# Un-normed inputs for the first projections and the query projection, and split passes for the retention products, in a two-block fp32 kernel

## The chip, the cores and the metric

One core of a Trainium2 chip. The metric is the time of one launch in device microseconds (us), the median of three runs. Engines are called by the profile's names: PE (TensorE), ACT (ScalarE), DVE (VectorE), POOL (GpSimd), SP (SyncE, which here only issues transfers).

## The reference

256 tokens of width 1024 go through two blocks. Cut to what the change touches:

```python
# first block
n1 = rmsnorm(h, norm1_g)                 # h / sqrt(mean(h*h) + eps) * gain
q, k, v, r, a_lr, su, sv, ga, gb = split(n1 @ w_in)
...                                      # gated linear attention, spatial gating, merge
h = h + merged @ w_out
n2 = rmsnorm(h, norm2_g)
q = (n2 @ w_q)                           # 8 heads x 2 halves x 128
s1, s2 = q[:, :, 0] @ sub_k1.T, q[:, :, 1] @ sub_k2.T
...                                      # top 16 of each, top 16 of the sums, experts, h = h + peer(n2)
# second block: two feed-forward layers around a retention layer with 4 heads
sc = einsum('id,jd->ij', q, k) * decay   # 256 queries, 512 keys (context and own), d = 256
o  = einsum('ij,jv->iv', sc, v)          # v is 512 wide
```

## The kernel before, in words

All weights are one stream of chunks of 128 x 1024 fp32 (512 KB), in the order of the table `ORDER`. SP loads chunk c into one of four slots of RAW (`load`, L372). A product with fp32 operands is computed in three passes: each operand is the sum of a part rounded to `float32r` (names with H) and the rest (names with L), and PE adds H*H, H*L and L*H (`product`, L1555 to L1557). So each chunk is split before use: ACT rounds it (`split_hi`, WH, L479) and DVE subtracts (`split_lo`, WL, L944; from the query projection to the experts POOL does it instead, `pool_lo`, L427). `split_hi(c)` waits for chunk c-4 on PE, `split_lo(c)` for `split_hi(c)`, SP's next load of the slot for `split_lo`. Every engine runs its own list in order and waits on semaphores; there is no planner.

A `feature_chunk` (24 matmuls with 256 columns) has the weights stationary and gives 128 features of 256 tokens, accumulated in one PSUM bank over the eight 128-row blocks k. A `token_chunk` (12 matmuls with 512 columns, L1586 to L1588) has the tokens stationary; four of them fill K, V or the gating input SV in token direction. A third form, in the experts, doubles the columns.

**Norm.** ACT squares the eight blocks (L482), PE sums them with a matrix of ones in eight plain fp32 matmuls (`norm_sum`, L1595), ACT takes the root (L486), DVE the reciprocal (L949), and then block by block DVE scales (L952), ACT rounds (L493, XH) and DVE subtracts (L959, XL). The PE's first product needs block 0 of this.

**Start.** After the norm: chunk "alr" (features), twelve token chunks "tok" (K, V, SV), then 28 feature chunks "feat" with pieces of the attention between them (`glu`). **Query projection.** "wout" (8 feature chunks, in a loop, each added to H by DVE), norm, "wq" (16 feature chunks in four loop rounds, each evicted to QT, then two small fp32 matmuls, `scores`, L1696), then "pre" (32 expert rows) beside a long top-k chain on DVE, whose result is turned by PE before the 29th of these chunks (L1743). **Retention heads.** Per head 14 chunks; between them eight plain fp32 matmuls with 256 columns for the scores (L1925), the decay on DVE (PT), and eight plain fp32 matmuls with 512 columns for the values (L1936).

## Time and profile before

| | us |
|---|---|
| median of 3 runs (lowest, highest) | 2168.5 (2166.01, 2171.08) |
| profiled execution, its own time | 2167.95 |
| its span, first to last instruction | 2166.1 |
| PE busy | 2101.8 (97%) |
| DVE, ACT, POOL busy | 1198.6, 1019.0, 132.2 |
| mean granted clock of PE | 0.99 |

The span is what the rows below are measured in; 1.85 us lie around it. PE's matmuls are pipelined: a row's duration reaches beyond the start of the next, so the step from start to start is what one costs. An idle time in brackets is that of the engine just before the row, with what ended it.

### The profile page before, as it was taken

To read this page: it belongs to the slowest core of one execution; us is meant where nothing else is said; L and a number is where in the kernel's file an instruction comes from. 1 tells how busy PE (TensorE), PEld (TensorE's weight loads), DVE (VectorE), ACT (ScalarE), POOL (GpSimd) and SP (SyncE) were. 2 spreads that over 40 slices of the span, in tenths; PEclk is the share of its full clock that TensorE was granted. 3 is DMA by queue.
4 is the path that set the end of the run, shared out by engine and by line. 5 is a ranking of instruction groups with operands and counts; after the bars stand their busy time and mean duration, and the time that the engine had idled before them with its cause. 6 is when DMAs were issued, how large, how long until landed. Compare 5 with 4: busy or idle time off the path is not lost.

```text
span 2166.1 us, 35548 instructions
## 1 busy us (share of the span) xinstructions
PE 2101.8 (97%) x12650; PEld 1825.6 (84%) x12650; DVE 1198.6 (55%) x2044; ACT 1019.0 (47%) x1538; POOL 132.2 (6%) x72
## 2 busy tenths in 40 slices
PE   8999998899999999999999999999999999999997
PEld 6899898778888888888888888887888888899996
DVE  4456794796666666666665333224544534355554
ACT  4644444675555555555554222213433434336753
POOL 0000567100000000000000000000000000000001
PEclk9999999999999999999999999999999999999999
DMA  6435356696555555565552233322323335254563
GB/s 214 138 127 175 117 204 207 237 324 222 191 191 187 189 186 189 189 204 191 187 167 102 96 95 96 115 95 75 107 88 116 97 137 184 88 190 140 182 195 117
DMA packets 95232, 343.91 MB, mean 159 GB/s; under 512 B 10962, under 2 KB 11474, under 8 KB 94772
## 3 DMA queue, kind: packets, MB, share of 16 engines
q1 hardware_dynamic: 93908, 337.28, 46.9%
q0 software_dynamic: 1248, 5.57, 0.7%
q8 instruction: 53, 0.87, 0.2%
q14 instruction: 23, 0.19, 0.0%
HBM read 341.76 MB, written 1.05 MB: 158 GB/s over the span
## 4 chain that ended last, share of the span: by engine, by line
PE 91%; DVE 3%; DMA 3%; ACT 2%; POOL 1%; issue 1%; ACTq 0%; DVEq 0%; POOLq 0%
PE ps L1555 15%; PE ps L1557 15%; PE ps L1556 15%; PE ps L1783 8%; PE ps L1797 5%; PE ps L1799 5%; PE ps L1798 5%; PE ps L1785 4%; DMA RAW<-in_wstream 3%; PE ps L1586 2%; PE ps L1587 2%; PE ps L1588 2%; PE ps L1761 2%; PE ps L1936 1%; PE ps L1719 1%; PE ps L1595 1%
## 5 line engine op out<-in xcount | busy, mean ns | idle before, releaser
L944 DVE TENSOR_TENSOR WL<-RAW,WH 128x1024 fp32r<-128x1024 f32 x517 | 624.6, 1223 | 492.9 <-ACT WH L479 486.9
L479 ACT ACTIVATE WH<-RAW 128x1024 fp32r<-128x1024 f32 x565 | 585.0, 1053 | 318.3 <-PE ps L1557 119.9
L1555 PE MATMUL ps<-XH,WH 128*128 128x256 f32 (+1 forms) x1200 | 385.4, 321 | 5.3 <-DVE XL L961 3.5
L1556 PE MATMUL ps<-XL,WH 128*128 128x256 f32 (+1 forms) x1200 | 379.8, 316 | 0.0
L1557 PE MATMUL ps<-XH,WL 128*128 128x256 f32 (+1 forms) x1200 | 379.7, 316 | 0.0
L1783 PE MATMUL ps<-XHL,WH 128*128 128x512 f32 x752 | 268.6, 397 | 0.0
L1555 PEld LDWEIGHTS ps<-XH,WH 128*128 128x128 f32 x1200 | 229.7, 191 | 24.0 <-DVE XL L961 3.9
L1556 PEld LDWEIGHTS ps<-XL,WH 128*128 128x128 f32 x1200 | 230.0, 192 | 15.5 <-issue 1.0
L1557 PEld LDWEIGHTS ps<-XH,WL 128*128 128x128 f32 x1200 | 229.9, 192 | 14.5
L1555 PE MATMUL ps<-XHL,WH 128*128 128x256 f32 x696 | 205.8, 296 | 19.7 <-POOL WL L427 8.7
L1785 PE MATMUL ps<-XHL,WL 128*128 128x256 f32 x752 | 210.9, 280 | 0.0
L1797 PE MATMUL ps<-WH,AH 128*128 128x512 f32 x512 | 202.4, 395 | 0.0
L1556 PE MATMUL ps<-XHL,WH 128*128 128x256 f32 x696 | 201.0, 289 | 0.0
L1799 PE MATMUL ps<-WL,AH 128*128 128x512 f32 x512 | 200.9, 392 | 0.0
L1557 PE MATMUL ps<-XHL,WL 128*128 128x256 f32 x696 | 200.6, 288 | 0.0
L1798 PE MATMUL ps<-WH,AL 128*128 128x512 f32 x512 | 199.9, 390 | 0.0
L1783 PEld LDWEIGHTS ps<-XHL,WH 128*128 128x128 f32 x752 | 141.3, 188 | 33.8
L1555 PEld LDWEIGHTS ps<-XHL,WH 128*128 128x128 f32 x696 | 137.2, 197 | 28.3 <-issue 20.1
L1785 PEld LDWEIGHTS ps<-XHL,WL 128*128 128x128 f32 x752 | 141.8, 189 | 3.6
L1556 PEld LDWEIGHTS ps<-XHL,WH 128*128 128x128 f32 x696 | 138.0, 198 | 0.2 <-issue 0.2
L1557 PEld LDWEIGHTS ps<-XHL,WL 128*128 128x128 f32 x696 | 137.6, 198 | 0.0
L427 POOL TENSOR_TENSOR WL<-RAW,WH 128x1024 fp32r<-128x1024 f32 x48 | 119.2, 2496 | 192.2 <-ACT WH L479 192.2
(307 smaller groups left out, 3038.6 us busy)
## 6 DMA issues: line engine op xcount, KB each, us to landing
RAW<-in_wstream SPq DMA_DIRECT2D x637, 512.0 KB, 3.4
H<-in_xT SPq DMA_DIRECT2D x1, 1024.0 KB, 5.2
CTX<-in_ctxT POOLq DMA_DIRECT2D x1, 1024.0 KB, 7.2
HX<-in_ctxT POOLq DMA_DIRECT2D x1, 1024.0 KB, 6.0
DIST<-in_dist POOLq DMA_DIRECT2D x1, 1024.0 KB, 5.0
out<-Y SPq DMA_DIRECT2D x4, 256.0 KB, 3.0
MASK<-in_mask POOLq DMA_DIRECT2D x1, 512.0 KB, 3.9
DFTL<-in_dftl POOLq DMA_DIRECT2D x1, 512.0 KB, 3.8
```

Of the source, the lines that this page charges most:

```text
L427: pool.tensor_tensor(WL[:, c % 4, :], RAW[:, c % 4, :], WH[:, c % 4, :].bitcast(F32), ALU.subtract).then_inc(lo_ready, 1)
L479: act.activation(WH[:, slot, :], RAW[:, slot, :], ACT.Copy).then_inc(hi_ready, 1)
L944: dve.tensor_tensor(WL[:, slot, :], RAW[:, slot, :], WH[:, slot, :].bitcast(F32), ALU.subtract).then_inc(lo_ready, 1)
L1555: pe.matmul(dst, wh, xh, start=start, stop=False, skip_group_check=not check)
L1556: pe.matmul(dst, wh, xl, start=False, stop=False, skip_group_check=not check)
L1557: return pe.matmul(dst, wl, xh, start=False, stop=stop, skip_group_check=not check)
L1586: pe.matmul(dst, xh[:, k, t], WH[:, slot, w], start=(k == 0), stop=False)
L1783: pe.matmul(both, WH[:, c % 4, w], XHL[:, :, k, :], start=(k == 0), stop=(k == KB - 1), skip_group_check=True)
L1785: ins = pe.matmul(ps[:, e % 4, 0:T], WL[:, c % 4, w], XH[:, k, :], start=False, stop=(k == KB - 1), skip_group_check=True)
L1797: pe.matmul(dst, AH[:, e % 2, t], WH[:, c % 4, d], start=first, stop=False)
L1798: pe.matmul(dst, AL[:, e % 2, t], WH[:, c % 4, d], start=False, stop=False)
L1799: ins = pe.matmul(dst, AH[:, e % 2, t], WL[:, c % 4, d], start=False, stop=last)
```

## The change

1. The first chunks take the un-normed input: H times the gain, split at once into XRA (high part by ACT, rest by DVE), block by block between the first four chunk splits. The inverse root, a number per token, is turned into token direction by two tiny matmuls (`turn_inverse`, copied to RTOK) and applied as ACT's scale when K, V and SV are evicted. The token chunks come first; "alr" follows them and uses the normed input, which is made beside them. x is loaded in four quarters. PE begins with twelve matmuls of ones on ones.
2. The sum of squares: POOL adds the eight blocks (`add_squares`), PE sums once (`raw_sum`).
3. "wq" takes XRP, made the same way from H while "wout" runs; the scale is applied when the scores are evicted. The loops of wout and wq are written out. The normed input for the experts is made during wq.
4. In each retention head Q, K, V and the decayed scores are split and both products run in three float32r passes.

```diff
@@ ORDER, NORM_BANK
+    ("tok", 12),
     ("alr", 1),
-    ("tok", 12),
-NORM_BANK = (4, 4, 3, 4, 4, 0, 4, 0)
+NORM_BANK = (0, 7, 3, 4, 4, 0, 4, 0)
@@ POOL
+            def add_squares(n, done):
+                for k in range(1, KB):
+                    pool.wait_ge(s["norm_sq"], n * KB + k + 1)
...
+                    pool.tensor_tensor(TMP8[:, 0, :], TMP8[:, 0, :], TMP8[:, k, :], ALU.add).then_inc(s["sq_added"], 1)
+            add_squares(N_GLA, 0)
...
+            add_squares(N_PEER, KB - 1)
             pool.wait_ge(lo_ready, C0["wq"] + 2)
@@ ACT, start
+            for q in range(4):
+                act.wait_ge(s[f"x_landed{q}"], 16)
+                for k in range(2 * q, 2 * q + 2):
+                    act.activation(XRA[:, 0, k, :], H[:, k, :], ACT.Copy, scale=col("norm1", k)).then_inc(s["xra_hi"], 1)
+                split_hi(q)
             for k in range(KB):
                 norm_square(N_GLA, k, H, TMP8)
-            split_hi(0)
-            split_hi(1)
-            norm_root(N_GLA, RMS[:, :])
-            for k in range(KB):
-                norm_round(N_GLA, k, TMP8, XH)
-            for c in range(0, 13):
+            for c in range(2, 13):
                 split_hi(c + 2)
+                if c == 2:
+                    norm_root(N_GLA, RMS[:, :])
                 if c in (4, 8, 12):
...
+                    for tt in range(TT):
+                        ins = act.activation((KT, VT, SV)[n][:, tt, :], ps[:, 4 + 2 * (n % 2) + tt, :],
+                                             (ACT.Copy, ACT.Copy, ACT.Gelu_apprx_tanh)[n], scale=RTOK[:, 0, tt:tt + 1])
+                if 5 <= c < 9:
+                    for k in range(2 * (c - 5), 2 * (c - 5) + 2):
+                        norm_round(N_GLA, k, TMP8, XH)
@@ DVE, start
+            for c in range(2, 13):
                 split_lo(c + 2)
+                if c == 2:
+                    tokens_inverse(N_GLA, RMS[:, :])
+                if c == 4:
+                    tokens_copy(N_GLA, 1, 0)
+                if 5 <= c < 9:
+                    for k in range(2 * (c - 5), 2 * (c - 5) + 2):
+                        norm_scale(N_GLA, k, H, TMP8, RMS[:, :], lambda k: col("norm1", k))
+                        if k:
+                            norm_rest(N_GLA, k - 1, TMP8, XH, XL, None)
@@ ACT, wq
+            for i in range(16):
+                split_hi(C0["wq"] + i + 2)
+                if i in (3, 4):
+                    for k in range(5 * (i - 3), 5 + 3 * (i - 3)):
+                        norm_round(N_PEER, k, TMP8, XH)
+                act.wait_ge(chunk_done, C0["wq"] + i + 1)
...
+                if i == 0:
+                    norm_root(N_PEER, RMS[:, :])
+                for done in ((), (), (), (0, 1), (2, 3))[i] if i < 5 else (i - 1,):
+                    scores(done)
@@ PE, start
+            for i in range(12):
+                pe.matmul(ps[:, 7, 0:P], ONES[:, :], ONES[:, :], start=True, stop=True)
+            for c in range(12):
...
+                token_chunk(c, part, 4 + 2 * (n % 2), TT, XRAH, XRAL, parts=s["xra_lo"] if c < 4 else None)
+                if c == 2:
+                    raw_sum(N_GLA)
+                elif c == 4:
+                    turn_inverse(N_GLA, 1, 0)
+            feature_chunk(C0["alr"], ps[:, 3, 0:T], XH, XL, norm=N_GLA)
@@ PE, wq
+            for i in range(16):
+                bank_free(U_WQ + i)
+                feature_chunk(C0["wq"] + i, ps[:, (U_WQ + i) % 4, 0:T], XRP[:, 0, :, :], XRP[:, 1, :, :],
+                              parts=None if i else s["xrp_lo"])
+                if i == 0:
+                    raw_sum(N_PEER)
+                elif i == 2:
+                    turn_inverse(N_PEER, 7, T)
+                if i:
+                    scores(i - 1)
+            scores(15)
@@ PE, heads
                 for jt in range(4):
                     for d in range(2):
-                        ins = pe.matmul(ps[:, jt // 2, (jt % 2) * T:(jt % 2) * T + T], KR[:, d, jt * P:jt * P + P],
-                                        QR[:, d, :], start=(d == 0), stop=(d == 1))
+                        keys = slice(jt * P, jt * P + P)
+                        ins = product(ps[:, jt // 2, (jt % 2) * T:(jt % 2) * T + T], KH[:, d, keys], KL[:, d, keys],
+                                      QH[:, d, :], QL[:, d, :], d == 0, d == 1)
...
-                pe.wait_ge(s["p_ready"], at(2, 1, it))
-                pe.wait_ge(s["v_ready"], at(1, 1, it))
+                pe.wait_ge(s["p_lo"], at(1, 1, it))
+                pe.wait_ge(s["v_lo"], at(1, 1, it))
...
-                        ins = pe.matmul(ps[:, 4 + tt, :], PT[:, jt, tt * P:tt * P + P], VR[:, jt, :],
-                                        start=(jt == 0), stop=(jt == 3))
+                        rows = slice(tt * P, tt * P + P)
+                        ins = product(ps[:, 4 + tt, :], PTH[:, jt, rows], PTL[:, jt, rows], VH[:, jt, :], VL[:, jt, :],
+                                      jt == 0, jt == 3)
```

Where the rows moved. ACT's list from the last chunks of wout into wq; L479 is `split_hi`, L482 the squares, L486 the root, L493 `norm_round`, L598 the eviction to QT. Before:

```order
L482 ACTIVATE TMP_81<-H 128x256 x8
L486 ACT_TABLE_LOAD
L486 ACTIVATE RMS<-ps,EPSC 128x256
L493 ACTIVATE XHL<-TMP_81 128x256 x8
...
L479 ACTIVATE WH<-RAW 128x1024
...
L598 ACTIVATE QT<-ps 128x256
```

and now, where L512 is `split_hi`, L515 a square, L519 the root, L526 `norm_round`, L631 the rounding to XRP, L646 the eviction of scores, L658 that to QT:

```order
L631 ACTIVATE XRP<-H,CL 128x256
L515 ACTIVATE TMP_82<-H 128x256
L512 ACTIVATE WH<-RAW 128x1024
L658 ACTIVATE QT<-ps 128x256
L519 ACT_TABLE_LOAD
L519 ACTIVATE RMS<-ps,EPSC 128x256
...
L512 ACTIVATE WH<-RAW 128x1024
L526 ACTIVATE XHL<-TMP_82 128x256 x5
L658 ACTIVATE QT<-ps 128x256
L646 ACTIVATE SC<-ps,RTOK 128x128 x4
L512 ACTIVATE WH<-RAW 128x1024
L526 ACTIVATE XHL<-TMP_82 128x256 x3
```

The root and the eight roundings, which all stood ahead of the first wq chunk, now stand inside wq: the root behind the first eviction, five roundings ahead of the fourth, three ahead of the fifth.

DVE's list at the start of the program, after the first four chunk splits (L993 `split_lo`, L1013 `norm_scale`, L1020 `norm_rest`), which before had the reciprocal, the scales and the rests ahead of the third split:

```order
L1003 RECIPROCAL RMS<-RMS 128x256
L993 TENSOR_TENSOR WL<-RAW,WH 128x1024 x2
L1009 COPY RTOK<-ps 128x2
L993 TENSOR_TENSOR WL<-RAW,WH 128x1024
L1013 SCALAR_TENSOR_TENSOR TMP_82<-H,CL,RMS 128x256 x2
L1020 TENSOR_TENSOR XHL<-TMP_82,XHL 128x256
L993 TENSOR_TENSOR WL<-RAW,WH 128x1024
L1013 SCALAR_TENSOR_TENSOR TMP_82<-H,CL,RMS 128x256
L1020 TENSOR_TENSOR XHL<-TMP_82,XHL 128x256
L1013 SCALAR_TENSOR_TENSOR TMP_82<-H,CL,RMS 128x256
L1020 TENSOR_TENSOR XHL<-TMP_82,XHL 128x256
L993 TENSOR_TENSOR WL<-RAW,WH 128x1024
```

Two scales and two rests now stand between the split of one chunk and that of the next, four times over.

DVE's list in a head, from the split of the V chunks on (L1504 KL, L1508 VL, L1514 the decay, L1518 PTL):

```order
L1508 TENSOR_TENSOR VL<-ps,VH 128x2048
L992 REGISTER_ALU
L993 TENSOR_TENSOR WL<-RAW,WH 128x1024
L992 REGISTER_ALU
L993 TENSOR_TENSOR WL<-RAW,WH 128x1024
L1514 SCALAR_TENSOR_TENSOR PT<-ps,EF 128x1024
L992 REGISTER_ALU
L993 TENSOR_TENSOR WL<-RAW,WH 128x1024
L1518 TENSOR_TENSOR PTL<-PT,PTH 128x1024
```

VL is new ahead of two chunk splits, and PTL is new behind a third one, whose own high part ACT makes behind PTH.

## Rows read from the trace of the kernel before

**Rows 1.** The page of the whole program: span, and PE's share.

```profile
span 2166.1 us, 35548 instructions
...
PE 2101.8 (97%) x12650; PEld 1825.6 (84%) x12650; DVE 1198.6 (55%) x2044; ACT 1019.0 (47%) x1538; POOL 132.2 (6%) x72
```

**Rows 2.** The chain of waits (start, length, what), of 0 to 70 and 190 to 300 us.

```profile
0.76 5.19 DMA H<-in_xT
...
233.35 0.45 PE ps L1696 x4
```

**Rows 3.** Timeline of PE (start, busy, row [idle before <-releaser]), 5 to 57 us.

```profile
6.53 6.50 PE L1595 MATMUL ps<-TMP,ONES 128*128 128x256 f32 x16 [6.53 <-ACT TMP L482]
16.98 0.55 PE L1555 MATMUL ps<-XHL,WH 128*128 128x256 f32 x1 [3.95 <-DVE XHL L959]
...
22.61 0.39 PE L1586 MATMUL ps<-WH,XHL 128*128 128x512 f32 x1
...
55.05 0.39 PE L1588 MATMUL ps<-WL,XHL 128*128 128x512 f32 x1
56.64 1.95 PE L1615 MATMUL ps<-WA,ALR 17*128 17x512 f32 x4 [1.21 <-ACT SV L524]
```

**Rows 4.** Timeline of ACT and DVE at the start.

```profile
1.55 1.28 ACT L482 ACT_TABLE_LOAD   x1 [1.55 <-POOL ALR L410]
...
16.75 0.48 DVE L952 SCALAR_TENSOR_TENSOR TMP<-H,CL,RMS 128x256 f32<-128x256 f32 x1
...
17.15 0.42 DVE L959 TENSOR_TENSOR XHL<-TMP,XHL 128x256 fp32r<-128x256 f32 x1
...
22.31 1.23 DVE L944 TENSOR_TENSOR WL<-RAW,WH 128x1024 fp32r<-128x1024 f32 x1 [0.52 <-ACT WH L479]
...
25.61 1.06 ACT L479 ACTIVATE WH<-RAW 128x1024 fp32r<-128x1024 f32 x1 [1.43 <-PE ps L1588]
```

**Rows 5.** Timeline of POOL and of DVE, 322 to 337 us and the program's end.

```profile
324.26 5.41 POOL L427 TENSOR_TENSOR WL<-RAW,WH 128x1024 fp32r<-128x1024 f32 x2 [2.69 <-ACT WH L479]
...
2153.60 2.96 POOL L462 TENSOR_TENSOR HXT<-Y,HXT 128x512 f32<-128x512 f32 x2 [318.77 <-DVE Y L1504]
...
322.80 2.29 DVE L1178 TENSOR_TENSOR EQ<-IAU,IF 128x2048 uint32<-128x2048 uint32 x1
...
327.45 4.37 DVE L1178 TENSOR_TENSOR EQ<-IAU,IF 128x2048 uint32<-128x2048 uint32 x1
```

**Rows 6.** Timeline of PE around the second norm.

```profile
213.55 3.62 PE L1595 MATMUL ps<-TMP,ONES 128*128 128x256 f32 x16
221.03 0.55 PE L1555 MATMUL ps<-XHL,WH 128*128 128x256 f32 x1 [3.87 <-DVE XHL L959]
```

**Rows 7.** Windows: us, busy of PE, PEld, DVE, ACT, POOL, granted clock, DMA share, GB/s.

```profile
221.00:227.20 6.20, 6.17 (x26) 6.12 (x27) 4.71 (x13) 3.57 (x8) 0.67 (x1) 0.50 0.00 0
```

**Rows 8.** Timeline of ACT: first query eviction and first expert row's.

```profile
227.10 0.38 ACT L598 ACTIVATE QT<-ps 128x256 f32<-128x256 f32 x1 [0.74 <-PE ps L1557]
...
282.75 0.38 ACT L630 ACTIVATE G<-ps 128x256 f32<-128x256 f32 x1 [0.78 <-PE ps L1557]
```

**Rows 9.** Timeline of DVE at the top-k's end; the line that turns its result.

```profile
359.36 2.74 DVE L1185 TENSOR_TENSOR SEL<-VAL,GSUM 128x128 f32<-128x128 f32 x2
...
L1743 PE MATMUL ps<-IDP,SEL x6: 272/272/273, 378.7 to 379.2; 128*128 128x128 f32 x6
```

**Rows 10.** Timeline of PE and ACT in the second head, 1619 to 1641 us.

```profile
1619.26 3.61 PE L1925 MATMUL ps<-QR,KR 128*128 128x256 f32 x16
1622.52 0.47 PE L1555 MATMUL ps<-XH,WH 128*128 128x256 f32 x1
...
1634.23 7.03 PE L1936 MATMUL ps<-VR,PT 128*128 128x512 f32 x16
1640.69 0.68 PE L1555 MATMUL ps<-XH,WH 128*128 128x256 f32 x1
...
1619.46 1.88 ACT L845 ACTIVATE VR<-ps 128x2048 f32<-128x2048 f32 x1 [9.82 <-PE ps L1588]
```

More of the change, by code:

```diff
@@ L293, in build @@
         PT = sb("PT", [P, 4, T])
+        PTL = sb("PTL", [P, 4, T], place[0] - 4096, dt=F32R)
         ON = sb("ON", [P, TT, RV])
@@ L587, in _ @@
             merged_hi(KB - 1)
-            with act.Fori(0, 2) as it:
-                for j in range(4):
-                    split_hi(C0["wout"] + j + 2, it, 4)
-            norm(N_PEER, H, TMP8, RMS[:, :], XH, (ring_evac, lambda k: U_WOUT + k + 1))
-            def query(c, j, it):
-                act.wait_ge(chunk_done, at(c + 1, 4, it))
-                act.wait_ge(s["scores_ready"], at(j + 1, 4, it))
-                act.activation(QT[:, j, :], ps[:, (U_WQ + j) % 4, 0:T], ACT.Copy).then_inc(ring_evac, 1)
@@ new lines, in _, with scores @@
+            for m in range(KB):
+                split_hi(C0["wout"] + m + 2)
+                if m:
+                    raw_hi(m - 1)
+                    norm_square(N_PEER, m - 1, H, TMP8)
+            raw_hi(KB - 1)
+            norm_square(N_PEER, KB - 1, H, TMP8)
+            def scores(i):
+                act.wait_ge(s["scores_ready"], i + 5)
+                act.wait_ge(s["rtok_ready"], 2)
+                for tt in range(TT):
+                    ins = act.activation(SC[:, i, tt, :], ps[:, 4 + i % 4, tt * P:tt * P + P], ACT.Copy,
+                                         scale=RTOK[:, 1, tt:tt + 1])
+                ins.then_inc(s["sc_ready"], 1)
```

204 lines of the change are left out of this document (128 added, 76 removed).

## The prediction

> **What bounds the kernel now.** I read the page first: PE is busy for 97% of the span [rows 1], so only its idle time, its cheaper instructions and its clock can give anything. Then the chain of waits and PE's timeline, at the three places that the change touches.
>
> At the start x lands after 5.19 us [rows 2]. PE then sums squares from 6.53 for 6.50 us, where the same sixteen rows take 3.62 at the second norm [rows 3, 6], and its first weight matmul comes at 16.98, behind a wait of 3.95 [rows 3]. The token chunks go from 22.61 to 55.05: 144 matmuls, 143 steps, 0.227 us each, so 2.72 a chunk; then PE waits 1.21 for the eviction of SV [rows 3]. So the start is a chain, what follows is PE.
>
> At the second norm PE ends wout at 213.55, sums, waits 3.87 and has its first wq matmul at 221.03 [rows 6]. The next 6.2 us run at a granted 0.50 [rows 7], the 1.2 GHz level, after a time in which PE had stood idle. The first query eviction is at 227.10 and that of the first "pre" chunk at 282.75 [rows 8].
>
> In the heads PE has no wait around the two products. The step from the first score matmul to the next chunk is 3.26, from the first value matmul 6.46; their own rows are 3.61 and 7.03 long, and the four chunks between take 11.71, so 2.9 for a feature chunk [rows 10].
>
> **Heads.** Both products become 24 float32r matmuls, like those of a chunk. The scores then cost a feature chunk, 2.9 at most, in place of 3.26 to 3.61: a gain of 0.5. The values cost 24 x 0.227 = 5.45 in place of 6.46 to 7.03, where I take 6.85: a gain of 1.4. Times four heads that is 7.6 us (bounds 5.5 to 9.2).
>
> What must hide: ACT rounds Q, K and the scores, DVE subtracts four times. Prices: 1.06 for 128x1024 on ACT and 1.23 on DVE [rows 4], so 2.4 to 2.5 for VL (128x2048); VH costs what VR did, 1.88 [rows 10]. From the end of the V chunks, 1619.3: VH to 1621.3, VL to 1623.8, two chunk splits to 1626.2, decay to 1627.4. ACT's PTH to 1628.5, then its rounding of the next chunk to 1629.6, for which DVE waits (it stands ahead of PTL), 1630.8, PTL 1632.1. PE wants it after scores and four chunks, at 1619.3 + 2.9 + 11.5 = 1633.7. So 1.6 us are left, and the split of Q and K lies beside four 24-matmul V chunks of 5.4 us. I cost both at nothing. Behind PTL on DVE stand the splits for two later chunks, free in time. Without the cover each head would lose what PTL is late.
>
> **Start.** Of x the first quarter must land: between 2 us (a quarter of the 5.19 would be 1.3) and the whole's 5.95; I take 4. ACT's table load now follows it, 1.28, then two roundings (0.42 each, as DVE's subtraction L959), the rounding of chunk 0 (1.06), DVE's 1.23: PE starts at 8.4 instead of 16.98. One chunk at the lower clock (2 x 2.72) and two at the higher end at 19. But the third is followed by the new sum. ACT gets to the squares at 12.7 (three more rounds of 2 x 0.4 + 1.06) and ends them at 15.4. Then POOL's seven adds. No such add is in the trace; half of a 128x512 one (two in 2.96) is 0.74, a quarter of a 128x1024 one 0.6 [rows 5]; with a hand-over 0.83 each, 5.8.
>
> Beside DVE they cost more. Rows 5 show it: the same subtraction-like DVE instruction takes 2.29 alone (322.80) and 4.37 when it starts at 327.45 while POOL's own row runs to 329.67; 329.67 + 2.29 is its end. So one holds the other off for a whole instruction. The change puts seven POOL adds beside DVE's splits at the start, and DVE's scales and rests beside POOL's splits in wq; with such a hold-off the sum below is 19, without it 25.8. The Trainium skill states it as a rule against such a placement ("SBUF — State Buffer", section "Who interferes with whom"): a DVE instruction with two SBUF inputs contends with a GpSimd one that reads SBUF, and the later of them blocks until the other is through. By that rule the sum is 19, and the trace agrees with it at 4.37 against 2.29.
>
> Two chunk splits of 1.23 fall among the adds: the first add starts at about 14.5, the last ends at about 21.3. PE has waited 2.3 us for them. From there nine chunks of 2.72, the sum and the turn (0.7), and the alternation in the middle four: rounding 1.06, subtraction 1.23, scale 0.48, rest 0.42, scale 0.48, rounding 0.42 with hand-overs make 4.1 for each chunk against PE's 2.72, which is 5.5 over four, less a lead of 2: 3.5. Sum 50.0, with "alr" 52.9, with the first feature chunk 55.8. PE's gate product (L1615) thus begins at 55.8 behind one more chunk, which before began at 56.64 with that chunk still to come: 56.64 + 2.9 - 55.8 = 3.7 gained, and another 0.5 from a later wait for a split that stays but shrinks. **4.2 us** (bounds 1.5, adds at 1.2 and the clock low twice as long, to 9, no alternation and no wait for the sum).
>
> **Second norm and wq.** XRP is ready block by block: the last H block is added 0.75 after wout's end, rounded and subtracted 0.85 later, and PE needs it only for the last three of its first 24 matmuls, at 2.5. POOL's last add is done by then. So the first wq chunk ends at 213.55 + 2.9, and the one summing matmul adds 0.45, where before it ended at 227.0: 10.1 gained, all at the higher clock. Of the 55.65 us between the evictions of rows 8, 16 chunks and 16 scores (0.45, rows 2) explain 53.6; 2.05 are seams of the four loop rounds and go.
>
> Then what is given back. ACT's list holds the fourth query eviction behind five roundings, which wait for DVE's scales, and these for POOL's splits of 2.4 us (4.8 for two, less in rows 5 only for the hold-off). In times of the old trace: DVE's first scale at 224.6, blocked from 225.1 to 227.5, fifth scale 230.4, QT evicted at 231.2 where PE wanted it at 230.0 (1.3 lost); then the other three roundings, blocked once more by POOL to 235.8, QT at 237.5 against 234.65 (2.95 lost); then POOL's split of the eighth chunk, 0.7 late. I take 5.0 (bounds 0.3, no hold-off, and 9, where PE's idle gaps bring the lower clock as the 3.87 of rows 6 did). **7.2 us** stay.
>
> The top-k on DVE starts about 3 us later against the old trace, less the 4.2 from the start. Its end, 362.1, is wanted by PE at 378.7 [rows 9]; PE now comes 11.4 earlier, at 367, so 4 or more are left. Costed at nothing.
>
> **Sum.** 4.2 + 7.2 + 7.6 = 19.0. From the profiled execution's own 2167.95 that gives 2149.0; the median shown is 0.55 above that execution, so 2149.5.
>
> **The rivals.**
> - *No hold-off.* Short adds and 256-column scales may slip between each other. For: POOL's rows in wq were 2.4 beside most of the top-k. Against: rows 5. Then 2.1 more at the start and 4.7 in wq: 2142.7.
> - *The clock falls in wq.* A gap near 3 us beside a weakly filled 10 us; the fall of rows 7 came with 3.87 of idle. Half clock over 6.2 to 6.8 us costs 3.3: 2152.8.
> - *The split chain in the heads is late.* It has 1.6 us in hand, and if VL or PTH are dearer, the heads give nothing: 2157.
> - *The norm stays in the path.* Scores need the turned root before they can be evicted. If PE waits there for as long as the first wq chunk came late before, the 10.1 goes: 2159.6. Against it: QT has four slots and scores four banks.
> - *Slower.* The chain VH, VL, two splits, decay, PTH, PTL in each head. It ends slower than before by over 0.2% if PTL is late by more than (19.0 + 4.3) / 4 + 1.6 = 7.4 us in each head, by less if PE's clock falls in such a gap. At 9 us late: 2149.5 + 4 x 7.4 = 2179. Its rows would have to be twice as long as rows 4 and 10 say.
>
> **How the numbers follow.** Forecast 0.50, no hold-off 0.21, clock 0.15, heads late 0.07, norm in the path 0.03, slower 0.02, and 0.02 for a change within 0.2%. The range reaches from 2140 (no hold-off with the heads at their upper bound) to 2155 (clock fallen and the start at a worse bound); it leaves out the last four. A measurement of this kernel can tell about 0.2% from no change, 4.3 us. Faster by more than that 0.96, within 0.02, slower 0.02.
>
> **What would show it.** First token matmul near 8.4, a wait of PE for POOL's last add near 19, waits of PE for DVE's splits of chunks 9 to 11, "alr" ending near 53. No granted clock of 0.50 and no idle time at the second norm. Two PE waits in wq ahead of L1696's matmuls, on ACT's QT, of 1 and 3 us. DVE's scales in wq partly over 2 us long. Score and value rows of 2.9 and 5.4 with no PE wait before them. The forecast is wrong if PE waits for PTL, if the adds take over 1.2 each, or if DVE rows beside POOL keep their old length.

## The result, and the profile after

| | before | after |
|---|---|---|
| median, us (4 runs each, same chip) | 2169.43 | 2148.93 |
| lowest to highest | 2166.01 to 2171.08 | 2148.43 to 2153.9 |
| ratio, 95% interval | | 0.9905, 0.9888 to 0.9923 |
| profiled execution, own time | 2167.95 | 2149.38 |
| its span | 2166.1 | 2147.6 |

The change is about 1% faster; the forecast was 2149.5. (The 2168.5 that stands ahead as the median before is that of the first three of these four runs.) The page of the changed kernel, its line of engines and its chain, answers to [rows 1]:

```profile
span 2147.6 us, 35688 instructions
...
PE 2084.9 (97%) x12718; PEld 1820.1 (85%) x12718; DVE 1233.9 (57%) x2078; ACT 1037.9 (48%) x1585; POOL 145.6 (7%) x86
...
PE 88%; DVE 4%; DMA 3%; ACT 2%; POOL 1%; issue 1%; SPq 0%; ACTq 0%; DVEq 0%; POOLq 0%
```

PE's busy time fell by 16.9 and the span by 18.5: PE bounds this kernel as before, and nearly all of the gain is less or faster work on PE. The totals say no more than that; where the gain arose comes from marks at the same place of the program in both traces.

**The start.** PE's timeline after, against [rows 3] (columns: start, busy, row, and the idle time before it):

```profile
9.45 0.66 PE L1685 MATMUL ps<-WH,XRA 128*128 128x512 f32 x1 [3.02 <-DVE WL L993]
...
22.63 0.70 PE L1700 MATMUL ps<-TMP,ONES 128*128 128x256 f32 x2 [3.12 <-POOL TMP L439]
22.98 0.70 PE L1685 MATMUL ps<-WH,XRA 128*128 128x512 f32 x1
23.48 0.63 PE L1686 MATMUL ps<-WH,XRA 128*128 128x512 f32 x1
...
26.81 0.39 PE L1685 MATMUL ps<-WH,XRA 128*128 128x512 f32 x1
...
30.33 0.60 PE L1706 MATMUL ps<-ONES,RMS 1*128 1x2 f32 x4
```

The first weight matmul comes at 9.45 instead of 16.98. The sum waits 3.12 for POOL, and behind that wait the matmuls step by 0.43 instead of 0.23 until 26.8, which costs 1.6 to 1.7 us (L1706, at 30.33, is the turn of the inverse root, two chunks behind the sum). The granted clock of that window is 0.53, the lower of PE's two levels; the window behind PE's first wait, at 0.52, is another such fall (columns as in [rows 7]):

```profile
10.00:13.20 3.20, 3.20 (x9) 2.49 (x8) 2.61 (x5) 2.45 (x6) 0.00 (x0) 0.52 1.03 374
13.20:23.50 10.30, 7.18 (x32) 5.59 (x31) 4.05 (x5) 4.91 (x12) 7.08 (x9) 0.99 0.86 318
23.50:26.90 3.40, 3.40 (x10) 2.68 (x9) 1.69 (x2) 3.39 (x4) 0.00 (x0) 0.53 0.03 5
```

POOL's seven adds, which no trace had shown before, answer to [rows 5]: first their row, then their durations (shortest, median and longest, in ns), then DVE's two splits among them; below are two adds in wout:

```profile
15.27 7.31 POOL L439 TENSOR_TENSOR TMP<-TMP 128x256 f32<-128x256 f32 x7 [13.79 <-ACT TMP L515]
L439 POOL TENSOR_TENSOR TMP<-TMP x7: 721/738/1522, 15.3 to 21.9; 128x256 f32<-128x256 f32 x7
14.72 1.21 DVE L993 TENSOR_TENSOR WL<-RAW,WH 128x1024 fp32r<-128x1024 f32 x1
18.96 1.31 DVE L993 TENSOR_TENSOR WL<-RAW,WH 128x1024 fp32r<-128x1024 f32 x1 [3.02 <-ACT WH L512]
...
209.31 1.19 POOL L439 TENSOR_TENSOR TMP<-TMP 128x256 f32<-128x256 f32 x1 [1.68 <-ACT TMP L515]
212.19 0.74 POOL L439 TENSOR_TENSOR TMP<-TMP 128x256 f32<-128x256 f32 x1 [1.69 <-ACT TMP L515]
```

The seven take 7.31, or 1.04 each. An add with DVE idle takes 0.74. The first, which begins while the split of 14.72 still runs, takes 1.27, and one that meets the split of 18.96 takes 1.52; both end 0.6 us behind the end of that split. The add at 209.31 does the same: the DVE split beside it runs from 208.68 to 209.90, and the add ends at 210.50. The alternation of DVE and ACT shows in DVE's splits:

```profile
37.00 1.22 DVE L993 TENSOR_TENSOR WL<-RAW,WH 128x1024 fp32r<-128x1024 f32 x1 [0.92 <-ACT WH L512]
40.78 1.23 DVE L993 TENSOR_TENSOR WL<-RAW,WH 128x1024 fp32r<-128x1024 f32 x1 [1.10 <-ACT WH L512]
44.57 1.23 DVE L993 TENSOR_TENSOR WL<-RAW,WH 128x1024 fp32r<-128x1024 f32 x1 [1.10 <-ACT WH L512]
```

Their period is 3.79, against PE's 2.72 per chunk. The "gate product" (L1615 before, L1733 after) is PE's first product behind the two kinds of chunks, and serves as a mark below. It begins at 58.3 (56.64 before, with one chunk still to come). DVE's first split behind the gates starts at 67.63 instead of 69.20: the start gained 1.6 us, not 4.2.

**Second norm and wq.** ACT's evictions, against [rows 8]:

```profile
213.57 0.38 ACT L658 ACTIVATE QT<-ps 128x256 f32<-128x256 f32 x1 [0.51 <-PE ps L1654]
...
229.09 0.74 ACT L526 ACTIVATE XHL<-TMP 128x256 fp32r<-128x256 f32 x2
232.38 0.42 ACT L526 ACTIVATE XHL<-TMP 128x256 fp32r<-128x256 f32 x1 [2.55 <-DVE TMP L1013]
232.71 0.36 ACT L658 ACTIVATE QT<-ps 128x256 f32<-128x256 f32 x1
```

PE has its first matmul of wq at 210.63, where wout ends, and the first query eviction comes 2.9 later; before it came 13.55 after wout's end. Nothing is left of [rows 6, 7]: no wait for the norm, and no lower clock there. The eviction at 232.71 is the one that stands behind roundings that wait 2.55 for DVE. DVE and POOL in the same place, against [rows 5]:

```profile
220.61 3.71 DVE L1013 SCALAR_TENSOR_TENSOR TMP<-H,CL,RMS 128x256 f32<-128x256 f32 x2
224.25 0.41 DVE L1020 TENSOR_TENSOR XHL<-TMP,XHL 128x256 fp32r<-128x256 f32 x1
...
229.56 2.39 DVE L1020 TENSOR_TENSOR XHL<-TMP,XHL 128x256 fp32r<-128x256 f32 x1 [1.58 <-ACT XHL L526]
...
216.76 7.28 POOL L458 TENSOR_TENSOR WL<-RAW,WH 128x1024 fp32r<-128x1024 f32 x3 [1.16 <-ACT WH L512]
229.30 2.37 POOL L458 TENSOR_TENSOR WL<-RAW,WH 128x1024 fp32r<-128x1024 f32 x1 [5.26 <-ACT WH L512]
```

Two scales take 3.71 (0.87 in e3 below) and end just behind POOL's three splits: the first takes 1.17 and ends behind POOL's second split, the next 2.62 and ends behind its third; a rest takes 2.39 (the others 0.41), beside POOL's next. PE's waits there, 200 to 290 us (line waited for: total, times, longest):

```profile
PE ps L1819 <- ACT QT L658: 2.4, 1, 2.4
PE ps L1652 <- POOL WL L458: 1.6, 2, 0.9
```

The first pre eviction is at 270.67 against 282.75. The top-k is far from late: DVE has its result at 352.8, and PE takes it at 364.9 with no wait for it (378.7 in [rows 9]).

**Heads.** PE's timeline in the second head, against [rows 10]; the first and the last "..." stand for the product's other matmuls, the one between for the four feature chunks:

```profile
1606.69 0.28 PE L1652 MATMUL ps<-QH,KH 128*128 128x256 f32 x1
...
1609.68 0.28 PE L1653 MATMUL ps<-XL,WH 128*128 128x256 f32 x1
...
1621.08 0.40 PE L1652 MATMUL ps<-VH,PTH 128*128 128x512 f32 x1
...
1626.55 0.28 PE L1652 MATMUL ps<-XH,WH 128*128 128x256 f32 x1
1626.66 0.28 PE L1653 MATMUL ps<-XL,WH 128*128 128x256 f32 x1
```

No row has a wait before it. From a product's first matmul to the second one behind the product: scores 2.99 (3.57 before), values 5.58 (6.98). That is 2.0 a head. The transposes of ON confirm it over three heads: 1573.1 to 1751.4, 178.3 us, against 184.2.

**The ledger**, each gain from a mark in both traces:

| stretch | gained, us | of which |
|---|---|---|
| to DVE's first split behind the gate product | 1.6 | forecast 4.2 |
| from there to the end of wout (210.6, 213.55) | 1.4 | a granted clock of 0.50 for 3.4 us at 70.4, in the trace of before alone |
| to the first pre eviction | 9.1 | forecast 7.2: 10.6 at the norm, 1.5 given back in wq |
| to the select transposes | 1.7 | another such fall, at 343.4, in before alone |
| one-hot stage (105.6, 108.7) | -3.1 | scatter, see the last experiments |
| to the transposes of H, with the heads (1461.3, 1453.6) | 7.7 | forecast 7.6 |
| to the end | 0.1 | |
| sum | 18.5 | forecast 19.0 |

### The profile page after: what moved, and what is told of

Read it like the earlier page. It is cut to its first block, busy times and chain, and to the rows that moved or that the text cites. A ratio compares the mean times of both kernels' runs of the same rounds, so it can differ in the third digit from the quotient of the medians.

```text
span 2147.6 us, 35688 instructions
## 1 busy us (share of the span) xinstructions
PE 2084.9 (97%) x12718; PEld 1820.1 (85%) x12718; DVE 1233.9 (57%) x2078; ACT 1037.9 (48%) x1585; POOL 145.6 (7%) x86
## 4 chain that ended last, share of the span: by engine, by line
PE 88%; DVE 4%; DMA 3%; ACT 2%; POOL 1%; issue 1%; SPq 0%; ACTq 0%; DVEq 0%; POOLq 0%
PE ps L1652 15%; PE ps L1653 15%; PE ps L1654 15%; PE ps L1911 8%; PE ps L1925 6%; PE ps L1927 5%; PE ps L1926 5%; PE ps L1913 4%; DMA RAW<-in_wstream 3%; PE ps L1685 2%; PE ps L1686 2%; PE ps L1687 2%; PE ps L1889 2%; POOL WL L458 1%; ACT WH L512 1%; PE ps L1847 1%
## 5 line engine op out<-in xcount | busy, mean ns | idle before, releaser
L993 DVE TENSOR_TENSOR WL<-RAW,WH 128x1024 fp32r<-128x1024 f32 x517 | 624.9, 1223 | 407.3 <-ACT WH L512 401.3
L512 ACT ACTIVATE WH<-RAW 128x1024 fp32r<-128x1024 f32 x565 | 585.5, 1053 | 280.2 <-PE ps L1927 106.7
L1913 PE MATMUL ps<-XHL,WL 128*128 128x256 f32 x752 | 210.9, 280 | 0.0
L1652 PE MATMUL ps<-XHL,WH 128*128 128x256 f32 x568 | 163.9, 289 | 11.2 <-POOL WL L458 8.4
L1911 PEld LDWEIGHTS ps<-XHL,WH 128*128 128x128 f32 x752 | 141.3, 188 | 33.8
L1653 PE MATMUL ps<-XHL,WH 128*128 128x256 f32 x568 | 161.4, 284 | 0.0
L1654 PE MATMUL ps<-XHL,WL 128*128 128x256 f32 x568 | 161.3, 284 | 0.0
L1913 PEld LDWEIGHTS ps<-XHL,WL 128*128 128x128 f32 x752 | 141.8, 189 | 3.6
L1652 PEld LDWEIGHTS ps<-XHL,WH 128*128 128x128 f32 x568 | 109.7, 193 | 18.5 <-issue 8.5
L1927 PEld LDWEIGHTS ps<-WL,AH 128*128 128x128 f32 x512 | 96.1, 188 | 23.2
L1925 PEld LDWEIGHTS ps<-WH,AH 128*128 128x128 f32 x512 | 96.1, 188 | 21.3
```

What stands on the lines that cost most here:

```text
L512: act.activation(WH[:, slot, :], RAW[:, slot, :], ACT.Copy).then_inc(hi_ready, 1)
L993: dve.tensor_tensor(WL[:, slot, :], RAW[:, slot, :], WH[:, slot, :].bitcast(F32), ALU.subtract).then_inc(lo_ready, 1)
L1652: pe.matmul(dst, wh, xh, start=start, stop=False, skip_group_check=not check)
L1653: pe.matmul(dst, wh, xl, start=False, stop=False, skip_group_check=not check)
L1654: return pe.matmul(dst, wl, xh, start=False, stop=stop, skip_group_check=not check)
L1911: pe.matmul(both, WH[:, c % 4, w], XHL[:, :, k, :], start=(k == 0), stop=(k == KB - 1), skip_group_check=True)
```

## The experiments

All medians stand against the kernel before in runs on the same chip. There are twelve runs, of which e11 and e12 repeat two kernels unaltered.

**e1: are the heads worth 7.6 by themselves?** The two products go back to plain fp32, as before the change, with the rest of the change in place.

```diff
-                        ins = product(ps[:, jt // 2, ...], KH[:, d, keys], KL[:, d, keys],
-                                      QH[:, d, :], QL[:, d, :], d == 0, d == 1)
+                        ins = pe.matmul(ps[:, jt // 2, ...], KR[:, d, jt * P:jt * P + P],
+                                        QR[:, d, :], start=(d == 0), stop=(d == 1))
...
-                act.activation(PTH[:, :, :], PT[:, :, :], ACT.Copy).then_inc(s["p_hi"], 1)
```

> The changed kernel with the retention heads as before: both products in plain fp32, without the splits of Q, K, V and the scores. Theory, cheaper instructions with all splits hidden: the time from the last one-hot matmul to the transposes of H at the second block's end was 1461.3 us before and 1453.6 after; here it is again 1461 to 1462, and the run is 7 to 8 us slower than the changed kernel, about 2156.7. Rival, part of the heads' gain is a luckier clock or waits elsewhere in that stretch: it comes back by 4 to 6 us only, 1458 to 1460.

Measured: 2156.25, ratio 0.9939 (0.9915 to 0.9964), against 0.9905 for the whole change. Up to the one-hot stage every mark is that of the changed kernel (gate product 58.5, select transposes 364.9). ON's transposes need 184.6 us over three heads, 61.5 each, as before the change; the rows are the old ones again:

```profile
1608.75 3.61 PE L2027 MATMUL ps<-QR,KR 128*128 128x256 f32 x16
...
1623.72 7.03 PE L2038 MATMUL ps<-VR,PT 128*128 128x512 f32 x16
1630.18 0.68 PE L1626 MATMUL ps<-XH,WH 128*128 128x256 f32 x1
```

So the heads' part of the change gives its 2 us a head, and nothing else. The stretch from the one-hot stage's end to the transposes of H came out 1463.8, longer than the 1461.3 of before: a fall of the clock at 1522.0 lasted 6.8 us here where it lasts 3.4 in the traces of before and after.

**e2: does POOL's sum of squares hold the start up?** PE sums all eight chunks, as before the change, but late, where the changed kernel has its sum.

```diff
-            add_squares(N_GLA, 0)
...
-                    raw_sum(N_GLA)
+                    norm_sum(N_GLA, TMP8)
```

> The changed kernel with the first norm's sum of squares by eight fp32 matmuls on PE behind the third token chunk, in place of POOL's seven adds and one matmul. Theory, the alternation of ACT and DVE in token chunks 7 to 11 sets when the start ends: PE no longer waits 3.1 us and keeps its clock (no 0.50 near 23 us), the sum ends at about 23.1 as now (19.5 + 3.6), and the gate product still begins at 58.3, within 0.7; PE waits more for DVE's splits instead. Rival, the wait for POOL and the 3.4 us at half clock behind it are what the start lost: the gate product begins 1.7 to 3 us earlier, at 55.3 to 56.6.

Measured: 2149.81, ratio 0.9908 (0.988 to 0.9936), the same as the changed kernel. No wait for POOL is left, but PE now does this at the same place, and the gate product comes at 57.2, 1.1 earlier:

```profile
20.13 3.62 PE L1692 MATMUL ps<-TMP,ONES 128*128 128x256 f32 x16
```

That lies between the theory (within 0.7 of 58.3) and the rival (1.7 to 3 earlier). 3.62 of PE's own work takes the place of a wait of 3.12, a sum of 0.7 and the slow steps behind it. The 1.1 did not last: falls at 69.4, 165.0 and 236.7 in this trace brought the first pre eviction to 273.1, 2.4 later than in the changed kernel.

**e4: is the warm-up with the matrix of ones worth its place?**

```diff
-            for i in range(12):
-                pe.matmul(ps[:, 7, 0:P], ONES[:, :], ONES[:, :], start=True, stop=True)
```

> The changed kernel without the twelve matmuls of ones at the start. Theory, the start waits for the squares' sum, whatever PE's clock did before: the first weight matmul stays at 9.45, the third token chunk ends later by 1 to 2.5 us (19.5 now), PE's wait for POOL shrinks from 3.1 by as much, and the gate product still begins at 58.3, within 0.7. Rival, the warm-up pays: the gate product begins 1.5 to 3 us later.

Measured: 2148.87, ratio 0.9893 (0.9863 to 0.9922). The first weight matmul is at 9.45 and the last one ahead of the sum begins at 19.17, 0.05 off the changed kernel's 19.12; the gate product comes at 58.5. The expectation that the third chunk would end 1 to 2.5 us later failed: with the warm-up and without it the first chunk's matmuls step by 0.43 until about 13.2. So the warm-up matmuls are worth nothing here.

**e5: is the alternation of ACT and DVE what holds the start?** In the chunks that carry the first norm's scales, DVE scales a pair before it splits the weights and subtracts the rests behind it.

```diff
             for c in range(2, 13):
+                if 5 <= c < 9:
+                    for k in range(2 * (c - 5), 2 * (c - 5) + 2):
+                        norm_scale(N_GLA, k, H, TMP8, RMS[:, :], lambda k: col("norm1", k))
                 split_lo(c + 2)
...
-                        norm_scale(N_GLA, k, H, TMP8, RMS[:, :], lambda k: col("norm1", k))
-                        if k:
-                            norm_rest(N_GLA, k - 1, TMP8, XH, XL, None)
-                if c == 8:
-                    norm_rest(N_GLA, KB - 1, TMP8, XH, XL, None)
+                        norm_rest(N_GLA, k, TMP8, XH, XL, None)
```

> The changed kernel with DVE's two scales moved ahead of the chunk's split in the middle four token chunks, and both rests behind it, so that ACT's roundings no longer wait for that split. Theory, the alternation costs the start: the period of DVE's chunk splits, 3.79 us now, falls to 2.8 to 3.1, PE's two waits of 0.77 for DVE's splits go, and the gate product begins 1.2 to 2 us earlier, 56.3 to 57.1. Rival, the waits only move, to the normed input that the alr chunk needs or to other splits: the gate product begins within 0.5 of 58.3.

Measured: 2148.54, ratio 0.9911 (0.9882 to 0.9941), but the gate product at 54.3, 4.1 earlier, where 1.2 to 2 were expected. DVE's splits, in the same stretch as above:

```profile
31.84 1.22 DVE L993 TENSOR_TENSOR WL<-RAW,WH 128x1024 fp32r<-128x1024 f32 x1 [1.55 <-ACT WH L512]
34.45 1.22 DVE L993 TENSOR_TENSOR WL<-RAW,WH 128x1024 fp32r<-128x1024 f32 x1
37.05 1.22 DVE L993 TENSOR_TENSOR WL<-RAW,WH 128x1024 fp32r<-128x1024 f32 x1
39.64 1.22 DVE L993 TENSOR_TENSOR WL<-RAW,WH 128x1024 fp32r<-128x1024 f32 x1
```

The period is 2.60 in place of 3.79, below PE's 2.72, and PE has no wait for a split left. But only part of the 4.1 is the alternation's. This trace also has no fall of the clock behind the wait for POOL's sum, which is 1.91 here. The kernel e7 below keeps the alternation, has a wait of 3.24 there and no fall either:

```profile
22.72 0.70 PE L1700 MATMUL ps<-TMP,ONES 128*128 128x256 f32 x2 [3.24 <-POOL TMP L439]
...
28.81 0.60 PE L1706 MATMUL ps<-ONES,RMS 1*128 1x2 f32 x4
...
56.81 1.98 PE L1733 MATMUL ps<-WA,ALR 17*128 17x512 f32 x4
```

From the sum to the turn e7 needs 6.09 and the changed kernel 7.70, so the fall costs 1.6. From the turn to the gate product both need 28.00, and e5 needs 25.55 (28.70 to 54.25). So the alternation holds 2.4 to 2.5 us, and the missing fall gave the other 1.6. In the marks 3.3 of the 4.1 are left at the select transposes (361.6 against 364.9); in the medians they do not show.

**e3: POOL's splits beside DVE's scales in wq.** DVE splits five of the query chunks itself; POOL begins at the next.

```diff
-            for c in [*range(C0["wq"] + 2, C0["pre"]), *C_PRE]:
+            for c in [*range(C0["wq"] + 7, C0["pre"]), *C_PRE]:
                 pool_lo(c)
...
             raw_lo(KB - 1)
+            split_lo(C0["wq"] + 2)
             tokens_inverse(N_PEER, RMS[:, :])
+            split_lo(C0["wq"] + 3)
+            split_lo(C0["wq"] + 4)
             tokens_copy(N_PEER, 7, T)
...
+                if k == 4:
+                    split_lo(C0["wq"] + 5)
             norm_rest(N_PEER, KB - 1, TMP8, XH, XL, None)
+            split_lo(C0["wq"] + 6)
```

> Edit: of the query projection's weight chunks, five splits (second to sixth chunk after the first two) go from POOL to VectorE, so that POOL is idle while VectorE scales the second norm's chunks. Theory (a long POOL split, 2.37 us, holds VectorE's short operations off until it ends: 3.71 us for the first two scales, 2.39 us for one rest): no scale (L1013's group) over 0.6 us and no rest (L1020's) over 0.6 us between the first query eviction and the first top-k; the eight normed chunks are ready about 2 us earlier in spite of 3 x 1.22 us of added splits on VectorE ahead of and 1 x 1.22 between them; TensorE's wait of 2.4 us for the fifth query's eviction falls below 1 us; first pre-gate eviction 1 to 2 us earlier against the gate product than now (212.3 us after it). Rival (ScalarE's list order alone makes the wait): rows may shorten, but the wait for the query stays at 2 us or more, since VectorE has 6 us more to do there; no gain, or up to 2 us lost. Either way the median moves by less than 3 us.

Measured: 2141.38 (2139.4 to 2143.76), ratio 0.9873 (0.9852 to 0.9894): the lowest median of the single edits, 7.5 us under the changed kernel's (6.9 by the ratios), where both theories had allowed 3. The intervals of the two ratios still touch (0.9888 to 0.9923 for the changed kernel); in the traces 6.1 us can be followed as far as the select transposes (358.8 against 364.9). DVE's groups by shape in 205 to 240 us (busy, mean ns), first the changed kernel, then e3:

```profile
L1013 DVE SCALAR_TENSOR_TENSOR TMP<-H,CL,RMS 128x256 f32<-128x256 f32 x8 | 6.6, 830 | 0.0
L1020 DVE TENSOR_TENSOR XHL<-TMP,XHL 128x256 fp32r<-128x256 f32 x8 | 5.3, 664 | 1.7 <-ACT XHL L526 1.6
```

```profile
L1013 DVE SCALAR_TENSOR_TENSOR TMP<-H,CL,RMS 128x256 f32<-128x256 f32 x8 | 3.8, 480 | 0.0
L1020 DVE TENSOR_TENSOR XHL<-TMP,XHL 128x256 fp32r<-128x256 f32 x8 | 3.4, 422 | 0.8 <-ACT XHL L526 0.8
```

With POOL idle no scale or rest is long any more, and DVE starts the top-k at 230.1 instead of 233.2 although it has 6 us more to do. From the first query eviction to the first pre eviction the window of the changed kernel, and that of e3:

```profile
213.60:270.70 57.10, 53.89 (x456) 52.96 (x455) 46.52 (x204) 36.38 (x76) 39.97 (x17) 1.00 0.44 149
```

```profile
213.90:267.10 53.20, 53.17 (x456) 52.77 (x456) 45.70 (x221) 36.40 (x76) 28.30 (x12) 1.00 0.48 160
```

PE is busy for 53.17 of 53.20 us: nothing waits any more. So the 3.9 us of stalls in wq came from POOL's splits, the 2.4 us for the eviction as well as the 1.6 for POOL's own weights. In 212 to 380 us PE's waits for POOL's splits fell from 7.8 to 4.6 too, which fits a POOL that enters the pre chunks with fewer splits behind it; the next stretch, to the select transposes, is 91.7 instead of 94.2.

**e7: or is it ACT's list alone?** The evictions and scores stand ahead of the roundings.

```diff
-                if i in (3, 4):
-                    for k in range(5 * (i - 3), 5 + 3 * (i - 3)):
-                        norm_round(N_PEER, k, TMP8, XH)
...
                     scores(done)
+                if i in (3, 4):
+                    for k in range(5 * (i - 3), 5 + 3 * (i - 3)):
+                        norm_round(N_PEER, k, TMP8, XH)
```

> Edit: in ScalarE's list the evictions of the fourth and fifth query chunk and the retention scores stand ahead of the roundings of the second norm, not behind. Theory (TensorE's 2.4 us wait is for the fifth query's eviction, queued on ScalarE behind roundings that wait for VectorE's scales, which POOL's split holds off): the wait for QT vanishes (below 0.5 us), the rows of 3.71 us (two scales) and 2.39 us (a rest) on VectorE stay, the first pre-gate eviction comes 1.5 to 2.5 us earlier against the gate product, the first top-k up to 1 us later. Rival (the projection's matmuls wait for something else, weights or banks, and this wait only covers it): a wait of like size for a weight split or bank turns up, gain below 0.5 us. Median 2146 to 2149 by the theory, if the clock lows stay where they are.

Measured: 2149.55 (2140.76 to 2151.3), ratio 0.9902 (0.9875 to 0.9929), no different from the changed kernel. The wait for QT is gone, DVE's scales still average 830 ns, and PE's waits for POOL took most of its place: 9.7 in 212 to 380 us, 7.8 before the edit. The stretch in wq went from 57.1 to 55.9, where 1.5 to 2.5 had been expected. Its gate product came at 56.8, though nothing is edited there: that is the missing fall shown under e5. So the eviction's place was one way in which POOL's splits reached PE, and their rate was the other.

**e6: the loop seams, in the kernel before.** Its wq loops on ACT and PE are written out.

```diff
-            with pe.Fori(0, 4) as it:
-                for j in range(4):
-                    bank_free(U_WQ + j, it)
-                    feature_chunk(C0["wq"] + j, ..., XH, XL, it, 4, norm=None if j else N_PEER)
+            for i in range(16):
+                bank_free(U_WQ + i)
+                feature_chunk(C0["wq"] + i, ..., XH, XL, norm=None if i else N_PEER)
```

> Edit on the kernel before: only the loops over the query chunks on ScalarE and TensorE are written out (16 copies in place of 4 x 4), arithmetic and order unchanged. The prediction priced the loop seams at 2.05 us of the middle's 7.2. Theory: the stretch from the first query eviction to the first pre-gate eviction, 55.65 us before, falls to 53.3 to 54.0 with the same clock low in it, and TensorE's gaps at the loop's turns (about 0.7 each) vanish. Rival (the seams are covered by a wait that ends at the same time, of weights or evictions): the stretch stays within 0.5 us and waits take the seams' place. Median 2165 to 2168 by the theory against about 2168 now.

Measured: 2167.12, ratio 0.9999 (0.9986 to 1.0012). The stretch from the first query eviction (226.8) to the first pre eviction (280.2) is 53.4 instead of 55.65: 2.25, where the seams were priced at 2.05. The profiled span is 2.7 shorter than before (2163.4); the median does not show it, and the interval, 2.8 us to either side, would hide it. With the seams 2.25 and 1.45 lost in the same stretch by the change, its stalls are 3.7, the 3.9 of e3's reading within 0.2.

**e8: both reorderings, e5 and e7.** Its diff is those two.

> Edit: two reorderings of the changed kernel together: at the start VectorE's scales of a pair of chunks stand ahead of the weight split, their rests behind it; at the second norm ScalarE's query evictions and scores stand ahead of the roundings. The first alone brought the gate product 4.0 us forward (54.3 against 58.3), the second is expected to bring 1.5 to 2.5. If they are independent: gate product at 54 to 55, first pre-gate eviction at 264.5 to 266 (270.7 now), end at 2141 to 2144. Rival (TensorE's granted clock takes it back: a fall to 0.50 of 3.4 or 6.8 us costs 1.7 or 3.4, and the one-hot stage's transfers are late by as much as the work before is early): marks up to the pre gates as above, but the end at 2145 or later.

Measured: 2145.82 (2141.65 to 2146.02), ratio 0.9892 (0.9874 to 0.991). Gate product at 54.3, first pre eviction at 266.9 rather than 264.5 to 266, with a fall of the clock of 3.4 us at 65.7, which costs 1.7. The start came out as in e5; the stretch in wq is 55.9, as in e7. The median is above the 2141 to 2144 expected.

**e9: e3 and e5 together. e10: with e7 on top.** No new edits.

> Edit: the two that each gave most, together: VectorE's scales ahead of the chunk split at the start (e5), and five query splits taken by VectorE in place of POOL (e3). Theory (independent losses in two stretches): gate product at 54.2 to 54.8 as in e5, from the first query eviction to the first pre-gate eviction 53.0 to 53.5 as in e3 (57.1 in the changed kernel), TensorE busy for over 53 of these; no VectorE scale over 0.6 us; end 3 to 4 us before e3's 2142.0 of span, 2137 to 2140 if the clock lows number no more than in e3. Rival (a gain of a few us is taken by the granted clock or by the one-hot stage's transfers): the marks up to the select transposes come forward by 4, the end by less than 2.

> Edit: as e9, and ScalarE's query evictions and scores ahead of the roundings (e7). Theory: e7's own gain was 1.2 of the 2.4 us waited, the rest went into more waits for POOL's weight splits; with the five splits off POOL and the scales no longer blocked, the rounding never holds the eviction up, so this edit is worth nothing here: within 0.3 us of e9 in every mark up to the first pre-gate eviction. Rival (the two add up): that stretch falls below 52.5 us. TensorE's own busy time there is 53.2, so the theory leaves no room for it.

Measured: e9 2140.1 (2133.99 to 2143.25), ratio 0.9862 (0.9839 to 0.9884); e10 2143.13 (2142.48 to 2144.09), ratio 0.9881 (0.9862 to 0.9901). In e9 the stretch in wq is 53.2 again; its gate product came at 56.2 and not at 54.3, with one more fall of the clock at 24.5, behind the wait for POOL's sum. That is 2.2 earlier than in the changed kernel, which has the same fall: the alternation's share alone.

In e10 the added edit was to be worth nothing, and it cost 3.4 us in its own stretch, which is 56.6 (the medians' intervals overlap). PE waits in 205 to 270 us (e10), and DVE's rows that explain them:

```profile
PE ps L1657 <- DVE WL L993: 3.0, 2, 2.0
...
218.16 0.87 DVE L1013 SCALAR_TENSOR_TENSOR TMP<-H,CL,RMS 128x256 f32<-128x256 f32 x2
223.22 0.43 DVE L1020 TENSOR_TENSOR XHL<-TMP,XHL 128x256 fp32r<-128x256 f32 x1 [4.19 <-ACT XHL L526]
```

The roundings now stand behind an eviction for which ACT waits on PE, DVE's first rest waits 4.19 for a rounding, and behind the rests on DVE stand weight splits that PE wants. Once DVE splits query weights, the roundings must come early; e7's order gained only where POOL does (1.2 us in its stretch).

**e11 and e12: the changed kernel and e9 once more, unaltered.**

> The changed kernel once more, unaltered, for the scatter of its stages. In its first profile the one-hot stage took 108.7 us (105.6 before) and TensorE ran at 0.50 from 10.0, 23.6, 146.5, 1525.5, 1948.7 and 2139.9 us. Theory (the stage's length is the rate at which the weight stream's transfers come in, and that differs between executions whatever the change is): the stage takes another length between 102 and 109, with the mean GB/s of that window moving the other way so that their product stays within 1%. Rival (the change fixes it, by the shifted start of the stage): 108 to 109.5 again, at 289 to 291 GB/s. All marks up to the select transposes within 2 us of the first profile, differences there being whole falls of the granted clock.

> The combination e9 once more, unaltered. Median expected 2138 to 2143, ratio to the kernel before within 0.985 to 0.988; from the first query eviction to the first pre-gate eviction 53.2 again, since TensorE fills it; the one-hot stage, 102.5 in its first profile, at another length between 102 and 109 if its rate is a matter of the execution, at 102 to 103 if this version fixes it.

Measured: e11 2148.56 (2145.77 to 2152.91), ratio 0.9914 (0.9881 to 0.9946); e12 2142.57 (2139.91 to 2144.81), ratio 0.9875 (0.9845 to 0.9905). The one-hot stage of the same program in its first profile and in e11's:

```profile
379.20:487.90 108.70, 99.40 (x1027) 74.18 (x1028) 96.28 (x280) 76.89 (x171) 1.08 (x1) 1.00 0.85 290
```

```profile
379.40:483.10 103.70, 98.69 (x1028) 74.61 (x1028) 95.82 (x280) 77.28 (x171) 1.17 (x1) 1.00 0.86 305
```

108.7 at 290 GB/s and 103.7 at 305: the same bytes in another time. PE's waits say where: in this stage it waited 5.9 us for the weight stream in the first profile and 1.5 in e11, which is 4.4 of the 5.0. e9's stage was 102.5 with 1.9 of such waits, and e12's, the same program, 108.3 with 6.7. Up to the select transposes e11 agrees with the first profile to 0.3 us. So the 3.1 us that the ledger books against the change lie within the scatter of one program, and a difference of this size between two single spans shows nothing. What sets the rate in an execution stays open.

## Why the prediction came out right

The mechanism and the total were right, 2149.5 against 2148.93; but two of the three terms were off, the start by 2.6 too high and the middle by 1.9 too low, and that these nearly cancel is luck.

- **Heads, 7.6: right.** Measured 2.0 a head, 7.7 in all, and e1 takes it back. 0.58 came from the scores and 1.40 from the values, where 0.5 and 1.4 were taken. The cover held: VL began at 1608.80 and took 2.29, PTL began at 1617.71 and took 1.22, so it ended at 1618.9, and PE took the values up at 1621.08. That is 2.1 us in hand where the prediction found 1.6.
- **Start, 4.2: measured 1.6.** The gate product was late by 2.5 (58.33 against 55.8). First, the adds ended at 22.6 and not 21.3: 1.3 lost. The first add began at 15.27, not about 14.5, since ACT came to the squares at 14.41 and not at 12.7: the first quarter of x landed at 4.99 and not at 4, and ACT waited 0.75 for a weight chunk. (PE too began late, at 9.45 and not 8.4, but the first three chunks still ended at about 19.4, close to the 19 of the forecast.) And the seven took 7.31, not 6.8: 0.74 and a hand-over of 0.14 each where 0.83 was taken for both, and 1.3 for the two splits among them where 1.0 was. Second, a step was missing: the clock fell behind the wait of 3.12, 1.6 us. That the wait caused it is not shown, for e7 had a longer one and no fall. Third, the sum, the turn and the slower steps behind each cost 1.3, not 0.7. Fourth, the alternation cost PE 2.4 and not 3.5, because its period was 3.79 and not 4.1: 1.1 the better way. 1.3 + 1.6 + 0.6 - 1.1 is 2.4, within 0.1 of what was lost. The place named for the loss, the alternation, was right, and e5 shows its size.
- **Hold-off.** The traces bear it out for long operations: 3.71 for two scales beside POOL, 0.87 without (e3); 2.39 for a rest, 0.42 without. They do so for short ones too: each add that begins beside a DVE split ends 0.6 behind that split. The Trainium skill ("SBUF — State Buffer", "Who interferes with whom") says that the later of two such instructions blocks until the other is through; those rows agree.
- **Second norm, 10.1: measured 10.6**, all at a granted clock of 1.00. **Seams, 2.05: measured 2.25** (e6).
- **Stalls in wq, 5.0: measured 3.7 to 4.0.** The forecast had waits of 1.3 and 2.95 for QT and 0.7 for POOL. There was one of 2.4 for QT and two of 1.6 together for POOL: the first rounding group was not blocked as the old times had suggested, because POOL's three splits ended at 224.0, and the fourth query was evicted at 226.88 with no wait of PE for it. By the prediction's own sign, two PE waits on ACT's QT of 1 and 3 us, this step was half right. e3 shows the cause as stated, and e7 that ACT's order alone is not it.
- **Top-k, costed at nothing: right.** Its result was there 12 us before PE took it, where the prediction had 4 or more.
- **Sum.** The terms measured 1.6 + 9.1 + 7.7 = 18.4 against 19.0. Beside these stood two things that no term had and that are not shown to be the change's: falls of the clock in the profile of before that the one of after had not (3.1 gained), and the one-hot stage (3.1 lost). They cancelled. That the 0.5 us between forecast and median is so small is luck; the interval of the ratio alone is over 7 us wide.
- **The rivals.** "No hold-off" fell by e3 and by the durations of the adds. The clock did not fall in wq, though it did at the start, where no rival had it. The heads were not late, the norm left the path, and nothing was slower.

**A version that beats both.** e9 ran twice, at 0.9862 (0.9839 to 0.9884) and 0.9875 (0.9845 to 0.9905) of the kernel before; the changed kernel's were 0.9905 (0.9888 to 0.9923) and 0.9914 (0.9881 to 0.9946). The medians are 8.8 and 6.0 us under the changed kernel's, and the first pair of intervals does not overlap; the second does. e3 alone has 0.9873 (0.9852 to 0.9894). What e5's reordering adds to e3 shows in the marks (gate product 56.2 in e9 and 58.7 in e3, both with the fall of the clock near 24; 54.2 in e12 without it), not in the medians.

## What to carry to other kernels

When work is taken off the critical path and laid beside other work, price it there and not alone: two 0.48 us scales on DVE took 3.71 us together instead of 0.87 beside 2.4 us splits on POOL, and the cure was to give DVE more work (five splits, 6 us) so that POOL had none beside it. Look for an alternation of two engines of which each waits for the other's last piece: batching the short steps took its period from 3.79 to 2.60 us and gave 2.4 us. Before a gain is put down to an edit, look whether another trace without the edit has it too: 1.6 of the 4.1 us of e5 were a fall of the clock that also failed to come in e7. And let no single span stand for a gain of 2 or 3 us: compare marks up to the stage in question, and note falls of the clock between them.
